# Moving the V-row accumulation of a gathered expert row from the end of its own step to behind the next step's dot product

## What is computed

```python
u = jnp.take(u_tab, idx, axis=0)
act = jax.nn.gelu(jnp.einsum('thkd,td->thk', u, hb), approximate=False)
w = (gate * act).astype(hb.dtype)
return jnp.einsum('thk,thkd->td', w, jnp.take(v_tab, idx, axis=0))
```

## Time and profile before

| | |
|---|---|
| time, median of 3 runs | 4540.91 us (4526.17 to 4541.5) |
| the profiled execution | 4531.58 us |
| its span, first to last instruction | 4529.8 us |
| mean granted TensorE clock | 0.941 of full speed |
| VectorE busy | 2757.8 us (61%) |
| TensorE busy | 3720.5 us (82%) |
| POOL busy | 789.4 us (17%) |

### The profile page before, as it was taken

The page is one execution under the profiler, slowest core; times in us unless marked ns, Lnnn a source line. Parts: engine busy times, 40 slices in busy tenths (PEclk is TensorE's granted clock), DMA queues, the critical chain, the costliest instruction groups (busy, mean ns, idle before and its releaser), DMA issues. The chain is left out here.

```text
span 4529.8 us, 43181 instructions
## 1 busy us (share of the span) xinstructions
PE 3720.5 (82%) x15216; PEld 2380.2 (53%) x15216; DVE 2757.8 (61%) x3992; ACT 868.8 (19%) x2027; POOL 789.4 (17%) x525
## 2 busy tenths in 40 slices
PE   8999999999999989777599898520688887777776
PEld 3444469996755666664588785220334443222222
DVE  2332249200599999874767777789676675545544
ACT  1232220100112111242111221111212222212111
POOL 0000000000033333222211111234212222222121
PEclk9999999999999999889899999765899999999999
DMA  3112128788699999999999999998999999999998
GB/s 127 56 46 74 47 103 292 257 302 290 223 361 368 370 410 395 405 408 419 411 404 429 419 429 426 380 376 347 412 407 419 408 404 405 425 426 426 429 421 360
DMA packets 142767, 1530.85 MB, mean 338 GB/s; under 512 B 15312, under 2 KB 21584, under 8 KB 22096
## 3 DMA queue, kind: packets, MB, share of 16 engines
q0 software_dynamic: 73728, 1073.77, 57.0%
q1 hardware_dynamic: 66960, 444.62, 25.7%
q10 hardware_dynamic: 1984, 11.31, 0.7%
HBM read 1525.45 MB, written 4.19 MB: 338 GB/s over the span
## 5 line engine op out<-in xcount | busy, mean ns | idle before, releaser
L1607 PE MATMUL bank<-arena_h,wring 128*128 128x128 f32 (+4 forms) x7808 | 1534.2, 359 | 61.9 <-DMA wring<-in_w_in 22.6
L1607 PEld LDWEIGHTS bank<-arena_h,wring 128*128 128x128 f32 x7808 | 1161.4, 195 | 430.6 <-issue 151.7
L561 POOL DMA_INDIRECT arena_c<-in_peer_uv,arena_c x256 | 509.5, 1990 | 2672.7 <-DVE arena_o L1287 1432.8
L1278 DVE SCALAR_TENSOR_TENSOR arena_c<-arena_c 128x2048 f32<-128x2048 f32 x256 | 585.8, 2288 | 204.0 <-DMA arena_c<-in_peer_uv,arena_c 203.8
L1287 DVE SCALAR_TENSOR_TENSOR arena_o<-arena_c,arena_o 128x2048 f32<-128x2048 f32 x256 | 601.2, 2348 | 67.8 <-ACT arena_c L749 62.3
L747 ACT ACTIVATE arena_c<-arena_c 128x1 f32<-128x1 f32 x384 | 77.9, 203 | 2049.3 <-DVE arena_c L1278 1538.3
L1931 PE MATMUL bank<-arena_c,arena_h 128*128 128x512 f32 x768 | 360.2, 612 | 125.6 <-ACT arena_h L912 125.6
L1896 PE MATMUL bank<-arena_c 128*128 128x512 f32 x768 | 350.8, 600 | 66.9 <-ACT arena_c L870 66.5
L1519 DVE SCALAR_TENSOR_TENSOR arena_c<-arena_c 128x2048 f32<-128x2048 f32 x96 | 220.1, 2292 | 234.1 <-DMA arena_c<-in_peer_uv,arena_c 233.9
L574 POOL DMA_INDIRECT arena_c<-in_peer_uv,arena_c x192 | 201.5, 1050 | 758.6 <-PE bank L1931 371.6
L1931 PEld LDWEIGHTS bank<-arena_c,arena_h 128*128 128x128 f32 x768 | 139.8, 192 | 345.7 <-ACT arena_h L912 204.3
(11 more groups left out here) (214 smaller groups left out, 2840.0 us busy)
## 6 DMA issues: line engine op xcount, KB each, us to landing
wring<-in_w_in SPq DMA_DIRECT2D x208, 1024.0 KB
wring<-in_gla_w_o SPq DMA_DIRECT2D x48, 1024.0 KB
wring<-in_conv_w_pw SPq DMA_DIRECT2D x48, 1024.0 KB
wring<-in_w_out SPq DMA_DIRECT2D x48, 1024.0 KB
wring<-in_peer_w_q SPq DMA_DIRECT2D x48, 1024.0 KB
wring<-in_w_v SPq DMA_DIRECT2D x16, 1024.0 KB
arena_c<-in_peer_uv,arena_c POOLq DMA_INDIRECT x448, 11.6
arena_h<-in_x_t SPq DMA_DIRECT2D x4, 1024.0 KB, 10.1
```

The source lines that it names most:

```text
L561: pool.indirect_dma_start(out=first_row[s], out_offset=None, in_=uv_tab, in_offset=at)\
L1278: V.scalar_tensor_tensor(row, row, 1.0, block_of(h2, n // P), ALU.mult, ALU.mult, accum_out=act_u[:, n % TOP:n % TOP + 1]).then_inc(dotted, 1)
L1607: last = M(ps[bank][:, at:at + hi - lo], w_tile(slot)[:, k, :], act_in[:, k, lo:hi], start=k == 0, stop=k == KT - 1)
```

## The change

The accumulation of step s - 1 is placed right behind the dot product of step s, ahead of the dense work of step s. The accumulation of the last step, and its handing on, come after the loop. Nothing else is changed: the same instructions, three slots, the same waits.

```diff
+            def hand_on(n):
+
+                if n >= STEPS - 3:
+                    dve.wait_ge(row_used, n + 1 + FIRST_SLOTS)
+                    dve.sem_inc(uv_used, 1)
...
                     dot(s)
+                    if s:
+                        add_row(s - 1)
+                        hand_on(s - 1)
                     beside(s)
                     if topk:
                         topk(k)
                     if k == COPY_AT:
                         indices(U + 1)
-                    add_row(s)
-                    if s >= STEPS - 3:
-                        dve.wait_ge(row_used, s + 1 + FIRST_SLOTS)
-                        dve.sem_inc(uv_used, 1)
+            add_row(STEPS - 1)
+            hand_on(STEPS - 1)
```

## The result

The changed kernel takes 4651.77 us (median of 4 runs, 4647.9 to 4653.25) against 4538.9 us: **1.0255 times as long, 95% interval 1.0241 to 1.0269**, 113 us slower. The forecast was 4593 us, in a range up to 4665: 61 us over the profiled execution, which it took as its base, and 54 over this median. The side was right and the time inside the range, but the loss is about twice the forecast one.

The account below looks back on a forecast made before the run. Bounds: VectorE and TensorE in convolution, bytes under full loads, VectorE and the slot loop nearly equal with gathers alone. Terms 34 + 15 + 8 + 4 = 61 us on the profiled 4531.6 gave 4593 us, range 4553 to 4665.

Parts of the forecast that it names:

- The wait for ScalarE goes: VectorE's accumulation finds its weight a whole step old; frees at most 62.3 us, only where no other wait takes it.
- The slot is freed later: Gather n+3 waits for accumulation n, now behind dot product n+1; two steps must hold 4.9 us + L.
- L: Time from POOL's start on a gather to the row's use; taken as 8.5 us without weights, up to 2.45 more with.
- L gets shorter: POOL's issue of a gather no longer meets a dot product: about 1 us, not 2.75; L from 10.6 to about 8.5.
- Item 1: Gathers alone, 49 steps: the slot loop lengthens the mean step from 6.1 to some 6.8 us, +34 us.
- Item 2: Full weight loads, 97 steps: some holes between gathers stay unfilled by weights, 0.15 us a step, +15 us; at most +48.
- Item 3: Convolution, 79 steps: only the steps shorter than 8.1 us lose, 0.1 us a step, +8 us, from 0 up.
- Item 4: Norm and merges, 33 steps: short steps stretch, +7, less 3 for ScalarE: +4 us, between -15 and +20.
- Rival B: Convolution: POOL gets in only after a train of dense instructions, L grows about 2.9 us; say 4655 us; chance 0.18.
- the forecast's own case: Whole kernel: the slot loop with a short L costs time, 4555 to 4640 us; chance 0.62.
- Rival A: Gathers land quicker, L at most 7.3 us with gathers alone: about 4497 us; chance 0.06 clearly faster, 0.14 within 0.5%.

Follow-up runs that it names:

- late issue: Kernel before, but POOL issues gather n only when dot product n-2 is done too; 4610.55 us against 4525.33, ratio 1.0181.
- split gathers: Each row gathered as two halves, each freed by itself: order of before 4491.36 us, new order 4501.36, with POOL's queue to match 4485.73; kernel before: ratios 0.9916, 0.9939, 0.9909.
- its own run: Kernel before with the new order in one stretch alone; against 4530.85 us: convolution 4537.51, norm and merges 4534.19, full loads 4599.13, gathers alone 4563.17.

## Why the prediction was right in kind and half the size

- *The wait for ScalarE goes, and is worth little.* Right: 62.3 us of waits are gone, and no stretch is shorter.
- *The slot is freed later; two steps >= 4.9 us + L.* Right. The 4.9 us measure 4.84 and 4.83, and VectorE waits for the row in 91 of the 96 steps under full loads, so the loop binds there. (That 4.84 and L add up to two steps is no proof by itself, since both are read between the same two starts.) The late issue shows the cause, and the split gathers show it by its absence.
- *L gets shorter, POOL's issue falls to about 1 us.* Right: 0.945 us mean under loads, 1.03 over the convolution. L with gathers alone is 8.0 us in the timeline above and 8.9 on average, where I took 8.5.
- *Item 1, gathers alone, +34.* Right: +32 in the stretch of the changed kernel, and +32 in its own run.
- *Item 2, full loads, +15. This is the term that failed.* It is +56 in the stretch and +68 in its own run. The step that failed reads "If weights fill every hole in the gathers nothing is lost" and "I take 0.15 x 97". The measured loss is 0.58 us a step, from 7.52 to 8.10. L under loads is 11.3 us on average and not near 8.5. That is above the top of my bound, 8.5 + 2.45 = 10.95, so the upper end of +48 was too low as well. I had looked at the balance of bytes, which says what a full queue can do, and took a value near it. But here the queue was full only while gathers were issued early enough, and the change took just that away: share 0.96, 391 GB/s. With half of the weights, where the DMA engines had time left (share 0.92), the loss in this stretch was the same 55 us.
- *Item 3, convolution, +8.* +16 in the stretch of the changed kernel, +7 in its own run; the same steps, left unchanged, differ by 7 us from trace to trace. VectorE's waits for rows rose from 14.0 us to 33.9, near the 20 or 30 named.
- *Item 4, norm and merges, +4.* +4, and +3 in its own run.
- *Rival B, POOL shut out by trains of dense work.* Wrong. In the convolution the issue starts 0.36 us into a train and takes 1.07 us:

```profile
1449.00 3.26 DVE L1314 SCALAR_TENSOR_TENSOR arena_c<-arena_c,cols 128x384 f32<-128x384 f32 x6
1449.36 1.07 POOL L561 DMA_INDIRECT arena_c<-in_peer_uv,arena_c  x1 [6.05 <-DVE arena_o L1287]
```

The total came near rival B's 4655 us by another road, and it lies inside the range by luck: the forecast's own case ended at 4640. Rival B's mark, an issue near 4 us, is missing, and its stretch is the wrong one.
- *Rival A.* Wrong side. The fit in the Trainium skill's "DMA: Bandwidth & Descriptors" (anatomy of one DMA on the GpSimd path) gives 6.8 us for this gather, as an estimate. The trace does not agree: with gathers alone the median from POOL's start to the landing is 8.1 us and the shortest 7.8, and the measurement decides.

## What to carry to other kernels

Where a ring of buffers is gone round by gather, use and release, write down the loop before moving a release: what must fit between which two uses, and the landing time *in the company that it will have*. That the engine has idle time, or that the DMA engines are full, says little: here they were full only because requests came early. And if one half of a buffer is done with sooner than the other, release it by itself; the same move that costs 2.5% with whole slots costs nothing that can be told with half ones and POOL's queue to match, and the halves by themselves gave 0.8%.

## What the runs showed of the hardware that was not expected

- POOL's issue of a gather takes 0.94 us beside an idle VectorE, 1.07 when it starts inside a train of 0.61 us instructions, and 2.75 to 2.99 when it starts just after a 2.3 us VectorE instruction on 128 x 2048 elements. That fits a lock that is held for one instruction and can be had between two. The Trainium skill's "SBUF — State Buffer" describes such a lock on the shared port pair, held for the whole instruction. For the writing of descriptors it names only VectorE's two-port modes; whether this float32 instruction uses one, no run shows, but it does delay the issue. In the late issue's timeline, one that starts 1.8 us earlier but inside such an instruction ended only 0.4 us earlier.
- Loading weight tiles of 1 MB on another queue, about one a step, lengthens a gather's median time to landing by 3.1 us (8.1 to 11.2), half tiles by 1.2 (9.3).
- Splitting the gathers seems to make a stretch faster that was not bound by late rows: steps 0 to 77 take 638.5 us in the order of before, where four traces with whole rows have 641.8 to 648.8. 256 more issues cost nothing that can be seen. Why is open. Smaller rows may let weight tiles through sooner, but no run tried that by itself.
- Halving the weights took 5 to 12 us off steps 0 to 77 in the order of before (636.6 us), so a few us there depend on the weight loads.
